# A two-layer conv and pooling trunk on eight cores: the channel LayerNorm's two sums in two column groups

## The reference

```python
h = x @ w_in                                       # 1024 -> 4608 columns
a_bg, a_cg, a_v, a_z, b_v, b_g, b_z, c_u, c_z = split(h)
y_a = a_bg * conv3(a_cg * a_v) * silu(a_z)         # mixer A
u_b = conv31(b_v * sigmoid(b_g))                   # mixer B, depthwise, causal
u_b = silu(layer_norm(u_b, ln_b_g, ln_b_b))        # over its 512 channels
y_b = u_b * silu(b_z)
p   = multiscale_causal_pool(c_u)                  # mixer C: windows 2, 4, 8, 16
y_c = (p @ pool_w + pool_b) * pool_scale * silu(c_z)
out = layer_norm(ALPHA * x + concat(y_a, y_b, y_c) @ w_out, ln_g, ln_b)
```

## Time and profile before

| | |
|---|---|
| median of 3 runs | 808.9 us (808.68 to 809.27) |
| the profiled execution | 809.2 us |
| its slowest core, first to last instruction | 807.7 us (core 3) |
| spans of the 8 cores | 802.9 to 807.7 us |
| PE busy | 785.7 us, 97% of the span, 5379 matmuls |
| DVE, ACT, POOL busy | 491.6, 394.7, 305.3 us |
| DMA | 104.04 MB, mean 129 GB/s |

### The profile page before, as it was taken

One profiled execution on the slowest core, in us unless ns is written; L12 is line 12 of the kernel. 1 busy time (PEld: TensorE's weight loads), 2 busy tenths in 40 slices (PEclk: granted clock), 3 DMA queues, 4 the chain that ended last, 5 costly groups with the idle time before them and its releaser, 6 DMA issues.

```text
span 807.7 us, 16527 instructions; the slowest of 8 cores (802.9 to 807.7 us)
## 1 busy us (share of the span) xinstructions
PE 785.7 (97%) x5379; PEld 416.7 (52%) x5379; DVE 491.6 (61%) x767; ACT 394.7 (49%) x646; POOL 305.3 (38%) x380
## 2 busy tenths in 40 slices
PE   7999999999999999999999989999999999999994
PEld 6566666654444444445555546666444444444442
DVE  1232368976565588456655638966556554897467
ACT  1222476554545785354555558435434347544431
POOL 4120168662100156347111017745601112773294
PEclk9999999999999999999999989999999999999998
DMA  8988789989666753754675669895557766532023
GB/s 119 164 150 162 175 113 159 156 118 195 157 140 164 176 120 53 93 75 80 154 160 123 171 139 182 120 143 80 81 147 165 179 155 192 88 53 40 1 87 122
DMA packets 59315, 104.04 MB, mean 129 GB/s; under 512 B 7232, under 2 KB 28224, under 8 KB 58720
## 3 DMA queue, kind: packets, MB, share of 16 engines
q0 software_dynamic: 29088, 61.26, 46.8%
q1 hardware_dynamic: 30144, 41.72, 18.7%
HBM read 116.52 MB, written 16.78 MB: 165 GB/s over the span
## 4 chain that ended last, share of the span: by engine, by line
PE 80%; DVE 7%; issue 4%; DMA 4%; ACT 2%; POOL 1%; SPq 0%; DVEq 0%; ACTq 0%; POOLq 0%
PE ps L555 49%; PE ps L1047 21%; PE ps L708 7%; DMA wrg<-w_in_r 3%; DVE mem L590 2%; DVE mem L585 2%; ACT mem L581 2%; DVE mem L772 1%; DMA mem<-mem 1%; PE pT L1139 1%; PE ps L947 1%; DVE mem L927 1%; PE ps L752 1%; PE ps L738 1%; DVE xT L590 1%
## 5 line engine op out<-in xcount | busy, mean ns | idle before, releaser
L555 PE MATMUL ps<-xT,wrg 128*128 128x384 bf16 (+6 forms) x2816 | 520.4, 340 | 4.8 <-ACT mem L581 3.7
L555 PEld LDWEIGHTS ps<-xT,wrg 128*128 128x128 bf16 x2816 | 272.3, 98 | 231.9 <-issue 17.9
L581 ACT ACTIVATE mem<-ps 128x512 f32<-128x512 f32 (+12 forms) x284 | 131.8, 485 | 173.7 <-PE ps L555 130.0
L1047 PE MATMUL ps<-wo,yb 128*128 128x512 bf16 (+1 forms) x792 | 184.3, 379 | 0.1
L585 POOL TENSOR_TENSOR yb<-mem 128x384 bf16<-128x384 f32 (+3 forms) x120 | 127.7, 1069 | 136.8 <-ACT mem L581 63.2
L496 POOL DMA_DIRECT2D wrg<-w_in_r x144 | 80.3, 560 | 205.5 <-PE ps L555 114.6
L1047 PEld LDWEIGHTS ps<-wo,yb 128*128 128x128 bf16 (+1 forms) x792 | 77.1, 98 | 89.9 <-issue 2.2
L581 ACT ACT_TABLE_LOAD x70 | 89.8, 1283 | 55.5 <-DVE mv L1085 42.0
L581 ACT ACTIVATE mem<-mem,par 128x384 f32<-128x384 f32 (+3 forms) x80 | 57.6, 728 | 80.2 <-DVE mem L585 74.8
L590 DVE SCALAR_TENSOR_TENSOR Rb<-Rb,ps 128x512 f32<-128x512 f32 (+1 forms) x60 | 41.1, 685 | 80.2 <-PE ps L1047 80.2
L590 DVE SCALAR_TENSOR_TENSOR mem<-mem,par 128x384 f32<-128x384 f32 (+3 forms) x80 | 65.2, 815 | 15.4 <-ACT mem L581 11.2
(11 more groups left out here) (61 smaller groups left out, 411.6 us busy)
## 6 DMA issues: line engine op xcount, KB each, us to landing
wrg<-w_in_r POOLq DMA_DIRECT2D x144, 256.0 KB, 6.2
mem<-mem SPq DMA_DIRECT2D x64, 135.0 KB, 3.5
Rb<-xin SPq DMA_DIRECT2D x16, 512.0 KB, 6.6
x1s<-Rb POOLq DMA_DIRECT2D x16, 512.0 KB, 3.7
Rb<-x1s SPq DMA_DIRECT2D x13, 512.0 KB, 5.4
mem<-mem SPq DMA_DIRECT2D x64, 103.0 KB, 5.6
wo<-w_out_r POOLq DMA_DIRECT2D x24, 256.0 KB, 8.7
out<-Rb POOLq DMA_DIRECT2D x8, 512.0 KB, 3.4
```

Of the source, the lines that this page charges most:

```text
L555: o = P.add("pe", lambda e, kk=kk: e.matmul(bk.ap[:, 0:N], lhsT=wrg_t[:, s, kk, :], rhs=xT(kk, tok0, N), start=(kk == 0), stop=(kk == 7)), ...
L581: return P.add("act", lambda e: e.activation(out=out, in_=in_, func=func, **kw), reads=reads, writes=writes, cost=cost).fin
L1047: o = P.add("pe", lambda e: e.matmul(Po.ap[0:n, :], lhsT=yb_t[:, ec, off:off + n], rhs=wo_t[:, ec, h * 512:(h + 1) * 512], start=(idx == 0 ...
```

## The change

It has three parts.

1. In `lnb` a group's sum and its sum of squares are made by two matmuls of 64 output columns each, one into partitions 0 to 63 of one bank, the other into partitions 64 to 127 of the same bank. They are issued in two bursts, groups 0 and 1, then 2 and 3, four matmuls each. All reading of PSUM comes after the last burst. The variance, the square root and the reciprocal work on the upper 64 partitions; the mean is written to both halves; a DVE copy brings 1/std to the lower half.
2. In every unit the first A group (not only in unit 0) rotates over A's own two `ua` buffers. The counter of the three goes on in groups 1 to 3.
3. In unit 2 the 12 output-weight loads are issued two at a time in the six steps of A groups 2 and 3.

```diff
         def new_ua(u, g):
-            i = rot("ua0", 2) if (u, g) == (0, 0) else rot("ua", 3)
+            i = rot("ua0", 2) if g == 0 else rot("ua", 3)
             return take((Z_UA, Z_UA + 2056, Z_UB)[i], F32, 514, 2)
...
-            def sqmm(g):
-                o = P.add("pe", lambda e: e.matmul(Pq.ap[:, 0:N], lhsT=ones_t[:], rhs=sqb[g].ap, start=(g == 0), stop=(g == 3)),
...
+            def sums(g):
+                for i, x in enumerate((cbs[g], sqb[g])):
+                    o = P.add("pe", lambda e, i=i, x=x: e.matmul(
+                        Ps.ap[64 * i:64 * i + 64, 0:N], lhsT=ones_t[:, 64 * i:64 * i + 64], rhs=x.ap, start=(g == 0), stop=(g == 3),
+                        tile_position=(0, 64 * i)), reads=[R_ones] + x.res, writes=Ps.res if (g, i) in ((0, 0), (3, 1)) else [],
+                        cost=mmc(N) / 2)
...
             yield f + 1.5
-            yield lambda: spare(2)
             Ps = yield from new_bank()
-            Pq = yield from new_bank()
-            for g in range(4):
-                o = P.add("pe", lambda e, g=g: e.matmul(Ps.ap[:, 0:N], lhsT=ones_t[:], rhs=cbs[g].ap, start=(g == 0), stop=(g == 3)),
...
-            sqmm(0)
-            f = sqmm(1)
-            yield f
-            act(m.ap, Ps.ap[:, 0:N], AF.Copy, Ps.res, m.res, scale=1.0 / 512, psum=True)
-            act(rs.ap, Ps.ap[:, 0:N], AF.Square, Ps.res, rs.res, scale=1.0 / 512, psum=True)
-            Ps.free()
+            sums(0)
+            f = sums(1)
             yield from square(2)
             f = yield from square(3)
             yield f + 1.5
-            sqmm(2)
-            f = sqmm(3)
+            sums(2)
+            f = sums(3)
             lnb_busy[0] = False
             yield f
-            f = stt(rs.ap, Pq.ap[:, 0:N], 1.0 / 512, rs.ap, ALU.mult, ALU.subtract, Pq.res + rs.res, rs.res, psum=True)
-            Pq.free()
+            lo, hi = slice(0, 64), slice(64, 128)
+            act(rs.ap[hi], Ps.ap[lo, 0:N], AF.Square, Ps.res, rs.res, scale=1.0 / 512, psum=True)
+            act(m.ap[lo], Ps.ap[lo, 0:N], AF.Copy, Ps.res, m.res, scale=1.0 / 512, psum=True)
+            f = act(m.ap[hi], Ps.ap[lo, 0:N], AF.Copy, Ps.res, m.res, scale=1.0 / 512, psum=True)
+            f = stt(rs.ap[hi], Ps.ap[hi, 0:N], 1.0 / 512, rs.ap[hi], ALU.mult, ALU.subtract, Ps.res + rs.res, rs.res, psum=True)
+            Ps.free()
...
+            P.add("dve", lambda e: e.reciprocal(out=rs.ap[hi], in_=rs.ap[hi]), reads=rs.res, writes=rs.res, cost=0.1 + 0.0064 * N)
+            f = P.add("dve", lambda e: e.tensor_copy(out=rs.ap[lo], in_=rs.ap[hi]), reads=rs.res, writes=rs.res, cost=0.1 + N * 0.0008,
+                      port=True).fin
...
-                    elif u == 2:
-                        load_wo(li, nt * g + t)
+                    elif u == 2 and g >= 2:
+                        load_wo(li, 2 * (nt * (g - 2) + t))
+                        load_wo(li, 2 * (nt * (g - 2) + t) + 1)
```

More of the change, by code:

```diff
@@ L735, in square @@
                 return act(sqb[g].ap, cbs[g].ap, AF.Square, cbs[g].res, sqb[g].res)
-            def sqmm(g):
-                o = P.add("pe", lambda e: e.matmul(Pq.ap[:, 0:N], lhsT=ones_t[:], rhs=sqb[g].ap, start=(g == 0), stop=(g == 3)),
-                          reads=[R_ones] + sqb[g].res, writes=Pq.res if g in (0, 3) else [], cost=mmc(N))
+            def sums(g):
[4 more added lines that the diff above has]
+                        cost=mmc(N) / 2)
                 sqb[g].free()
@@ L747, in lnb @@
             yield f + 1.5
-            yield lambda: spare(2)
             Ps = yield from new_bank()
-            Pq = yield from new_bank()
-            for g in range(4):
-                o = P.add("pe", lambda e, g=g: e.matmul(Ps.ap[:, 0:N], lhsT=ones_t[:], rhs=cbs[g].ap, start=(g == 0), stop=(g == 3)),
-                          reads=[R_ones] + cbs[g].res, writes=Ps.res if g in (0, 3) else [], cost=mmc(N))
-            sqmm(0)
-            f = sqmm(1)
-            yield f
-            act(m.ap, Ps.ap[:, 0:N], AF.Copy, Ps.res, m.res, scale=1.0 / 512, psum=True)
-            act(rs.ap, Ps.ap[:, 0:N], AF.Square, Ps.res, rs.res, scale=1.0 / 512, psum=True)
-            Ps.free()
+            sums(0)
+            f = sums(1)
             yield from square(2)
@@ L762, in lnb @@
             yield f + 1.5
-            sqmm(2)
-            f = sqmm(3)
+            sums(2)
+            f = sums(3)
             lnb_busy[0] = False
             yield f
-            f = stt(rs.ap, Pq.ap[:, 0:N], 1.0 / 512, rs.ap, ALU.mult, ALU.subtract, Pq.res + rs.res, rs.res, psum=True)
-            Pq.free()
+            lo, hi = slice(0, 64), slice(64, 128)
[4 more added lines that the diff above has]
+            Ps.free()
             yield f
-            f = act(rs.ap, rs.ap, AF.Sqrt, rs.res + [R_eps], rs.res, bias=eps_t[:, 0:1])
+            f = act(rs.ap[hi], rs.ap[hi], AF.Sqrt, rs.res + [R_eps], rs.res, bias=eps_t[hi, 0:1])
             yield f
-            f = P.add("dve", lambda e: e.reciprocal(out=rs.ap, in_=rs.ap), reads=rs.res, writes=rs.res, cost=0.1 + 0.0064 * N).fin
+            P.add("dve", lambda e: e.reciprocal(out=rs.ap[hi], in_=rs.ap[hi]), reads=rs.res, writes=rs.res, cost=0.1 + 0.0064 * N)
+            f = P.add("dve", lambda e: e.tensor_copy(out=rs.ap[lo], in_=rs.ap[hi]), reads=rs.res, writes=rs.res, cost=0.1 + N * 0.0008,
+                      port=True).fin
             left = [4]
```

## The result

The changed kernel takes 811.7 us (median of 8 runs), the kernel before 808.8 beside it: ratio 1.0035, 95% interval 1.0024 to 1.0046. I forecast 801.0, 799.0 to 805.2, and gave "slower" 5%. It is slower by 2.8 us by the ratio: little, but clear of the interval. (In some executions, of any of these kernels, four of the cores run at a lower granted clock and the time is longer; ratios and profiles here leave those out.)

The account below looks back on a forecast made before the run. TensorE, fed back to back nearly everywhere, was taken as the bound. Slowest core 1: 804.5 - 1.7 (unit 2 gap) - 3.3 (LayerNorm sums) = 799.5, plus 1.5 outside the span = 801.0 us; range 799.0 to 805.2.

Parts of the forecast that it names:

- slower: Outcome that the changed kernel takes longer than the one before; 5%, all from the rival of two stalls in rotation.
- -3.3: LayerNorm sums on PE: 7.0 us of slots saved, 4.2 paid for 20 bursts, 0.5 saved beside convs; on every core.
- PE has spare banks meanwhile ...: I count nothing.: LayerNorm tiles: added work, some 0.6 us on ACT and 0.5 on DVE per tile, stays hidden beside PE; cost 0.
- about 1 us for each of 10 tiles: LayerNorm tiles: price of the added ACT and DVE work if PE's spare banks did not cover it.
- 799.5: Forecast span of core 1, the slowest after the change: 804.5 - 1.7 (unit 2 gap) - 3.3 (LayerNorm sums), in us.
- A: Rival, unit 2: conv takes over the wait for input DMAs, landing no earlier; core 3 keeps 2.4 us, time 804.6; 13%.
- B: Rival, LayerNorm sums: pairs don't run together or weight loads stand bare; time 808.0, no change; 5%.
- C: Rival, units 1 to 3: buffer rotation stalls, added ACT and DVE work lengthening its wait; time 813.4, slower; 5%.
- D: Rival, unit 2: another reader of shared memory keeps the gap, only the LayerNorm part arrives; 805.9; 7%.

Follow-up runs that it names:

- e11: full-sum with each pair of sums in 64-column groups, without third reading or copy, every engine's order kept; 805.9 us, ratio 0.9989.
- e9: full-sum with only the third ScalarE reading and the DVE copy added, every engine's order kept; 810.7 us, ratio 1.0053.
- full-sum: Kernel before with parts 2 and 3, sums of 128 columns in two banks, issued as in the change and read after the last; 805.0 us, ratio 0.9959.
- e12: The whole change (64-column pairs, third reading, DVE copy), sums and squares in two banks, in full-sum's order; 809.1 us, ratio 1.0029.
- e10: The changed kernel in its own order, third reading and DVE copy cut to 2 columns each; 812.7 us, ratio 1.0075.
- e8: The changed kernel, planner told a full slot instead of half for each 64-column matmul: same instructions, another order; 817.3 us, ratio 1.0116.
- e2: Kernel before with parts 2 and 3 alone, the old sums; 803.9 us, ratio 0.9958.
- e3: Kernel before with part 2 alone, output weights loaded as before; 805.1 us, ratio 0.997.
- e4: The changed kernel in its planned order, the DVE copy of 1/std cut to 2 columns; 809.6 us, ratio 1.0033.
- e15: The changed kernel, order kept, the DVE reciprocal cut to 2 columns; 807.6 us, ratio 0.9999.

## Why the prediction was wrong

**Part 1 on PE: right.** The slots, summed over all matmuls of core 3, fall by 7 us; entering and leaving cost 0.21 us a burst, and about 0.1 is saved where a burst stands next to a conv (none of the 0.09 of entering is seen there). -3.3 was right as an account of PE. It was wrong to carry it to the end of the program "on the path, on every core": e11 shows that of 3.3 us nothing arrives. What takes it stands in unit 0: 7.3 us against 3.0 between 110 and 180, of which the mode changes are 0.6. The other 3.7 are waits for DVE and ACT, and PE's being early is only a small part of them: by my slots the three tiles of unit 0 save 1.8 us and pay 1.3 for six bursts, 0.5 us (an estimate). DVE and ACT themselves are later, as at 109 above.

**The step that failed: "PE has spare banks meanwhile ...: I count nothing."** The sizes were near: three readings of 0.59 us at 64 partitions instead of two at 128, and a copy that I put at 0.5 us and that is, at 512 columns, 0.42 at best and 1.17 in the mean (0.74 over all ten). The cover was not there. I had named the price of missing cover, "about 1 us for each of 10 tiles", and e9 measures 7.6 us for the ten, in full-sum's order; but it stood in no rival and had no chance of its own. I judged the cover by shares of the whole span (ACT 49%, DVE 61%). The stretch decides. Windows of 700 to 736 us on core 3, PE, weight loads, DVE, ACT, POOL, then clock: first full-sum (e5), then after:

```profile
700.00:736.00 36.00, 35.98 (x167) 16.15 (x166) 29.05 (x39) 16.40 (x28) 22.71 (x22) 1.00 0.37 52
```

```profile
700.00:736.00 36.00, 32.95 (x152) 14.76 (x151) 33.84 (x37) 14.81 (x27) 24.88 (x22) 0.98 0.36 52
```

DVE is 81% busy there in the good kernel (87% from 110 to 180 us, in unit 0); 33.84 of 36 us in the changed one. But the added work alone does not do that. The same window in e9, then in e12, which have it in full-sum's order:

```profile
700.00:736.00 36.00, 34.83 (x162) 15.62 (x161) 29.98 (x40) 14.27 (x25) 23.69 (x23) 1.00 0.39 61
```

```profile
700.00:736.00 36.00, 34.42 (x160) 15.33 (x158) 30.34 (x40) 15.36 (x26) 22.34 (x22) 1.00 0.36 58
```

The table has 1.5 and 2.5 us for them in unit 3 where the change has 5.7. So what follows is the chain in the change's own order, and most of this one place is the order's. How DVE came to be so late is seen further ahead. ACT and DVE after, core 3:

```profile
687.16 1.88 ACT L581 ACTIVATE mem<-ps 64x512 f32<-64x512 f32 x3 [3.69 <-PE ps L739]
...
695.00 0.72 ACT L581 ACTIVATE mem<-mem,epst 64x512 f32<-64x512 f32 x1
```

```profile
699.90 0.69 DVE L585 TENSOR_TENSOR mem<-ps,mem 128x512 f32<-128x512 f32 x1 [2.98 <-ACT mem L581]
700.51 0.16 DVE L594 COPY mem<-tailA 128x2 f32<-128x2 f32 x1
700.70 3.35 DVE L770 RECIPROCAL mem<-mem 64x512 f32<-64x512 f32 x1
704.15 0.42 DVE L771 COPY mem<-mem 64x512 f32<-64x512 f32 x1
...
723.49 4.72 DVE L590 SCALAR_TENSOR_TENSOR mem<-mem,par 128x512 f32<-128x512 f32 x2 [1.11 <-ACT mem L581]
```

And the same tile in full-sum (e5):

```profile
688.00 0.72 ACT L581 ACTIVATE mem<-mem,epst 128x512 f32<-128x512 f32 x1
```

```profile
691.65 3.34 DVE L772 RECIPROCAL mem<-mem 128x512 f32<-128x512 f32 x1
```

After, the three readings are at the head of ACT's list and hold it for 3.69 us until PE has made the burst; the square root comes 8.6 us behind the burst's start at 686.44, in full-sum 5.7 behind 682.30; DVE idles for ACT, and starts the reciprocal 14.3 us behind the burst instead of 9.4. Of ACT's 8.6 us the third reading is 0.6; between the last reading and the square root the planner has put five other activations and two table loads of 1.28 us. Eight products, the finishing of four groups and two groups of mixer C then stand behind it in a stretch where DVE has no time to give back, and the first L947 waits 3.05 us. A burst of 64-column matmuls is short on PE, but its reader is as long as ever and one longer.

**The order.** I held the planner's order to be fixed. Its costs changed (half slots, two new instructions, one bank less), and it moved far more than the sums: in unit 3, 26 projection groups instead of 25 lie between the last burst and the first L947. How much of the 6.5 us this is I can't say as one number: none to 1 us with the longer chain (after against e12), 6.9 us without it (e10 against e11), some 6 from a number of the plan alone (e8).

**Part 2: right, and part 3 did what it was for, though its worth in time isn't shown.** e2 brings 3.4 us by ratio; its slowest core is core 3 with 802.4 us, core 1 has 801.0. I had 799.5 + 3.3 = 802.8 for core 1 without part 1, 801.9 for core 3. The conv does not wait, the clock stays at 1.00.

**The rivals.** A's wait is in e3, smaller than I had it, and was taken away by part 3. B is excluded by the pairs. D is excluded by the gap that is gone. C had the right sign and nearly the size (813.4), but not the place: there is no wait of PE in unit 1 for the buffer rotation (300 to 375 us: 0.45 in all, the mode changes). No rival had the mechanism that came, ScalarE and VectorE late from phase A on; the 5% for "slower" stood on another one.

**Open.** The chain, the shorter PE time and the order interact. In full-sum's order each of the first two costs time by itself (e9, e11), and both together (e12) lose as much as the change does, so the new order isn't needed for the loss. In the change's order cutting the chain's two instructions short brings nothing (e4, e10), and that is not explained. e15 shows that DVE's load is not the whole: the split between ACT's held list and DVE's collisions with POOL was not measured.

The best of the kernels that leave nothing out is e2 with 803.9 us (0.9958), e5 the same within the interval: parts 2 and 3 without part 1, some 6 us by ratio below the change.

## What to carry to other kernels

An instruction moved or added "beside" the bottleneck engine is hidden only where its own engine has time to spare in that stretch: read the windows of the stretch, not the share of the span, and give "the cover isn't there" a chance and a price of its own. A saving on the bottleneck engine counts only as far as the others can follow; here 3.3 us less on PE brought nothing (e11), as DVE and ACT in unit 0 had no time to spare and became later. And where a planner writes the order, try a change in the frozen order as well as in its own, or its effect and that of the reshuffle can't be told apart.

## What the runs showed of the hardware

- Work on 64 partitions is no shorter than on 128: the reciprocal of 512 columns takes 3.35 us on either, ScalarE's reading of 512 from PSUM 0.59.
- An excursion to 64-column groups costs 0.21 us (0.09 in, 0.12 out), the same as one to 32-column groups (0.11 and 0.10).
- DVE instructions grow beside POOL's products. The ten copies of the change on core 3 (min/median/max ns):

```profile
L771 DVE COPY mem<-mem x10: 305/422/2899, 115.5 to 704.2; 64x384 f32<-64x384 f32 x4, 64x512 f32<-64x512 f32 x4, 64x288 f32<-64x288 f32 x1, 64x256 f32<-64x256 f32 x1
```

The one of 2.9 us lies under two POOL products of 1.2 us each; the five with none beside them take 0.42 at most. The Trainium skill says it in "SBUF — State Buffer", section "SBUF: two separate sides": the two engines take a common port in turn, each for a whole instruction, and on DVE's side a copy from SBUF to SBUF in fp32 is of that kind, or, against a GpSimd instruction that reads SBUF, an operation with two SBUF inputs. The trace agrees: the two products cover 2.6 of the copy's 2.9 us. I had priced the copy between two rows, one of 32 columns and one of two inputs, without asking what POOL does beside it.
